# One-hot products of the spread step in three bf16 parts instead of one float32 product, with tokens innermost

## The reference, cut to what matters

```
eid  = i1 * 128 + i2                      # 8 heads x 16 choices = 128 experts per token
gate = softmax(best_s)
act  = gelu(einsum('thkd,td->thk', u[eid], x))
out  = einsum('thk,thkd->td', gate * act, v[eid])
```

## Time and profile before

| what | before |
|---|---|
| median of 3 runs | 4023.95 us (4020.21 to 4025.05) |
| the profiled execution, its own time | 4031.59 us |
| its span in the profile | 4029.8 us |
| granted TensorE clock, mean over the span | 0.932 |
| busy: PE, weight loads, VectorE, ScalarE, GpSimd | 3728.5, 2386.4, 2323.1, 1266.1, 658.0 us |

### The profile page before, as it was taken

The page is one execution under the profiler, slowest core; times in us unless marked ns, Lnnn a source line. Parts: engine busy times, 40 slices in busy tenths (PEclk is TensorE's granted clock), DMA queues, the critical chain, the costliest instruction groups (busy, mean ns, idle before and its releaser), DMA issues.

```text
span 4029.8 us, 48913 instructions
## 1 busy us (share of the span) xinstructions
PE 3728.5 (93%) x14086; PEld 2386.4 (59%) x14086; DVE 2323.1 (58%) x4748; ACT 1266.1 (31%) x3367; POOL 658.0 (16%) x602
## 2 busy tenths in 40 slices
PE   7977999789999999997998899799589999999997
PEld 3443583576677777663444444347476677777764
DVE  1072696579877655664123400258978977755556
ACT  1141010357655454001011100101156755545201
POOL 0000001123433222220000000000113333311221
PEclk9988999669999999998997999899758999999998
DMA  3101148559999877993211112213657999977897
GB/s 131 64 20 52 63 169 362 198 204 388 379 392 400 342 298 299 396 383 133 73 63 47 42 73 73 84 61 120 258 188 289 386 377 394 391 300 301 343 384 284
DMA packets 129888, 926.81 MB, mean 230 GB/s; under 512 B 14800, under 2 KB 15744, under 8 KB 18184
## 3 DMA queue, kind: packets, MB, share of 16 engines
q0 software_dynamic: 73728, 536.90, 32.8%
q1 hardware_dynamic: 52368, 377.51, 24.4%
q10 hardware_dynamic: 3704, 11.36, 0.8%
HBM read 923.59 MB, written 2.12 MB: 230 GB/s over the span
## 4 chain that ended last, share of the span: by engine, by line
PE 86%; ACT 5%; DVE 5%; issue 2%; DMA 2%; ACTq 0%; DVEq 0%; POOL 0%; POOLq 0%; SPq 0%
PE proj L646 21%; PE proj L429 16%; PE obk L637 16%; PE tps L594 11%; PE proj L421 10%; PE proj L608 5%; ACT hot L920 2%; PE proj L578 2%; ACT hot L923 1%; DMA wring<-in_slabs 1%; PE tps L394 1%; PE obk L745 1%; DMA ring<-in_experts,idx 1%; DVE stat L1186 0%; PE proj L735 0%
## 5 line engine op out<-in xcount | busy, mean ns | idle before, releaser
L646 PE MATMUL proj<-wring,hT 128*128 128x512 f32 x2048 | 943.3, 604 | 1.8 <-DVE hT L1391 1.8
L374 POOL DMA_INDIRECT ring<-in_experts,idx x512 | 635.5, 1241 | 1766.1 <-DVE xn L1365 1655.9
L637 PE MATMUL obk<-hT,wring 128*128 128x256 f32 x3072 | 694.2, 379 | 0.0
L637 PEld LDWEIGHTS obk<-hT,wring 128*128 128x128 f32 x3072 | 583.5, 190 | 159.5 <-issue 89.5
L594 PEld LDWEIGHTS tps<-hT,hot 128*128 128x128 f32 x4096 | 601.0, 226 | 123.6 <-ACT hot L923 61.0
L594 PE MATMUL tps<-hT,hot 128*128 128x32 f32 x4096 | 597.8, 304 | 74.7 <-ACT hot L923 49.4
L1365 DVE SCALAR_TENSOR_TENSOR xn<-ring,coef,xn 128x1024 f32<-128x1024 f32 x512 | 628.7, 1280 | 22.4 <-DVE coef L1355 1.2
L1348 DVE SCALAR_TENSOR_TENSOR ring<-ring,xn 128x1024 f32<-128x1024 f32 x512 | 601.0, 1221 | 7.7 <-DMA ring<-in_experts,idx 7.6
L646 PEld LDWEIGHTS proj<-wring,hT 128*128 128x128 f32 x2048 | 377.0, 192 | 379.4 <-issue 372.6
L429 PE MATMUL proj<-hT,wring 128*128 128x512 f32 x1280 | 561.0, 596 | 9.2 <-DMA ring<-in_keys 5.2
L920 ACT ACTIVATE hot<-iota_sb,table 128x128 f32<-128x128 f32 x1792 | 567.1, 390 | 2.5 <-issue 1.3
(11 more groups left out here) (228 smaller groups left out, 2134.5 us busy)
## 6 DMA issues: line engine op xcount, KB each, us to landing
wring<-in_slabs SPq DMA_DIRECT2D x356, 1024.0 KB
ring<-in_experts,idx POOLq DMA_INDIRECT x512
x_res<-in_x SPq DMA_DIRECT2D x1, 2048.0 KB, 9.9
ring<-in_keys ACTq DMA_DIRECT2D x2, 1024.0 KB, 6.9
out<-x_res SPq DMA_DIRECT2D x4, 512.0 KB, 2.6
ring<-ada_rows ACTq DMA_DIRECT2D x1, 1536.0 KB, 6.3
ring<-in_norm_pre ACTq DMA_DIRECT2D x2, 512.0 KB, 7.2
ring<-ada_rows ACTq DMA_DIRECT2D x1, 1024.0 KB
```

Source lines behind the costliest of these rows:

```text
L374: pool.indirect_dma_start(rows[:, r, :], None, d[f"experts{layer + 1}"], bass.IndirectOffsetOnAxis(idx[:, k, r:r + 1], 0)).then_inc(row[r] ...
L637: m = pe.matmul(obk[:, j % 2, 0:DT], wring[:, k, at + c * P:at + (c + 1) * P], hT[:, c, GB * P:T], start=(c == 0), stop=(c == DC - 1))
L646: m = pe.matmul(proj[:, 2 * b + c, :], coef_t[:, j % 2, b * P:(b + 1) * P], wring[:, k, at + c * 512:at + (c + 1) * 512], start=False, sto ...
```

## The change

The spread's one matmul in float32 per token becomes three in bf16 that add up in PSUM. The one-hots are exact in bf16; the gate is split into three bf16 numbers whose sum is the float32 gate (`gate_parts`). Keys, gate parts and `iota` are kept in bf16; `iota8` is `iota` repeated for eight tokens. All one-hot tiles are laid out with the eight tokens innermost, so a token's weights and columns are read at a step of eight bf16 elements (16 bytes). `hot2` gets two buffers of a whole group instead of two single halves. In the lone spread VectorE writes all of `hot2`; in the chunks ScalarE still does, with eight activations into a step of 16 bytes and one relu over 1024. `key_numbers` now reads its iota out of `iota8`, at that same step. The diff, cut to its core:

```diff
-SG = 4
+PARTS = 3
-HOT2 = SGROUPS + (CHUNKS - 1) * SGROUPS * 2
+HOT2 = (CHUNKS - 1) * SGROUPS
...
-        table = sb("table", [P, 4, DT])
-        hot2 = sb("hot2", [P, 2, SG, NK])
+        iota8 = sb("iota8", [P, NK, TG], BF16)
+        keys = sb("keys", [P, 2 + PARTS, DT], BF16)
+        away = sb("away", [P, DT])
+        hot2 = sb("hot2", [P, 2, NK, TG], BF16)
...
-        hot1 = hT[:, 4:6, 0:TG * CK].rearrange("p k (t n) -> p k t n", t=TG)
+        hot1 = hT[:, 4:4 + PARTS, 0:TG * CK].bitcast(BF16).rearrange("p c (k n t) -> p c k n t", k=2, t=TG)
+        onehot1 = hT[:, 7, 0:TG * CK].bitcast(BF16).rearrange("p (k n t) -> p k n t", k=2, t=TG)
...
+                if hot2_count is not None:
+                    pe.wait_ge(hot2_ready, hot2_count)
                 pe.wait_ge(spread_free, grp + 1)
-                for half in range(2):
-                    if hot2_counts[half] is not None:
-                        pe.wait_ge(hot2_ready, hot2_counts[half])
-                    for t in range(SG):
-                        at = (half * SG + t) * CK
-                        m = pe.matmul(tps[:, k, at:at + CK], hot2[:, half, t, :], hot1[:, k, half * SG + t, :], start=True, stop=True)
-                    m.then_inc(spread_done, 1)
+                for t in range(TG):
+                    for c in range(PARTS):
+                        m = pe.matmul(tps[:, k, t * CK:(t + 1) * CK], hot2[:, k, :, t], hot1[:, c, k, :, t],
+                                      start=(c == 0), stop=(c == PARTS - 1))
+                m.then_inc(spread_done, 1)
...
-            def hot2_half(layer, c, g, half, token, count):
-                act.wait_ge(spread_done, g * 2 + ((layer * CHUNKS + c) * SGROUPS * 2 + half + 3))
-                for t in range(SG):
-                    i = act.activation(hot2[:, half, t, :], iota[:, :], ACT.Abs, bias=table[:, 3, bass.ds(token + (half * SG + t), 1)])
+            def hot2_group(layer, c, g, k, token, count):
+                act.wait_ge(spread_done, g + ((layer * CHUNKS + c) * SGROUPS + 1))
+                for t in range(TG):
+                    i = act.activation(hot2[:, k, :, t], iota8[:, :, t], ACT.Abs, bias=away[:, bass.ds(token + t, 1)])
                 i.then_inc(away_set, 1)
                 act.wait_ge(away_set, count)
-                act.activation(hot2[:, half, :, :], hot2[:, half, :, :], ACT.Relu, bias=1.0, scale=-1.0).then_inc(hot2_ready, 1)
+                act.activation(hot2[:, k, :, :], hot2[:, k, :, :], ACT.Relu, bias=1.0, scale=-1.0).then_inc(hot2_ready, 1)
...
                 with act.Fori(0, ROUNDS) as it:
-                        hot2_half(layer, 0, n, 1, token, n + (layer * HOT2 + 1))
                         spread_take(layer, 0, n, g % 2, token)
...
-                                hot2_half(layer, c + 1, tile, 0, token, made)
-                                hot2_half(layer, c + 1, tile, 1, token, made + 1)
+                                hot2_group(layer, c + 1, tile, j % 2, token, tile + (layer * HOT2 + c * SGROUPS + 1))
...
+            v.wait_ge(in_cst, 32)
+            v.tensor_copy(iota8[:, :, :], bcast(iota, 2, [P, NK, TG]))
             v.memset(silz[:, :, :], 0.0)
...
-                link(v.tensor_tensor(onehot, bcast(half_f, 3, grid), iota[:, 0:K].unsqueeze(1).unsqueeze(1).to_broadcast(grid),
+                link(v.tensor_tensor(onehot, bcast(half_f, 3, grid), iota8[:, 0:K, 0].unsqueeze(1).unsqueeze(1).to_broadcast(grid),
...
+            def gate_parts(job):
+                for b in range(TB - GB):
+                    at = slice(b * P, (b + 1) * P)
+                    i = v.tensor_tensor(rest[:, at], tps[:, (job + b) % 2, 2 * P:3 * P], keys[:, 2, at], ALU.subtract)
+                link(i)
+                link(v.tensor_copy(keys[:, 3, :], rest))
+                link(v.tensor_tensor(keys[:, 4, :], rest, keys[:, 3, :], ALU.subtract))
...
-                v.wait_ge(spread_done, g * 2 + (first * 2 + 2))
-                v.tensor_tensor(hot1[:, k, :, :], iota[:, c * CK:(c + 1) * CK].unsqueeze(1).to_broadcast([P, TG, CK]),
-                                bcast(table[:, 0, tok], 2, [P, TG, CK]), ALU.is_equal).then_inc(hot1_set, 1)
+                v.wait_ge(spread_done, g + (first + 1))
+                v.tensor_tensor(onehot1[:, k, :, :], iota8[:, c * CK:(c + 1) * CK, :], bcast(keys[:, 0, tok], 1, [P, CK, TG]),
+                                ALU.is_equal).then_inc(hot1_set, 1)
                 if both:
-                    v.wait_ge(spread_done, g * 2 + (first * 2 + 3))
-                    v.tensor_tensor(hot2[:, 0, :, :], iota[:, :].unsqueeze(1).to_broadcast([P, SG, NK]),
-                                    bcast(table[:, 1, bass.ds(token, SG)], 2, [P, SG, NK]), ALU.is_equal)
+                    v.tensor_tensor(hot2[:, k, :, :], iota8[:, :, :], bcast(keys[:, 1, tok], 1, [P, NK, TG]), ALU.is_equal)
                 v.wait_ge(hot1_set, g + (first + 1))
-                v.tensor_tensor(hot1[:, k, :, :], hot1[:, k, :, :], bcast(table[:, 2, tok], 2, [P, TG, CK]),
-                                ALU.mult).then_inc(hot_ready, 1)
+                v.tensor_tensor(hot1[:, :, k, :, :], bcast(onehot1[:, k, :, :], 1, [P, PARTS, CK, TG]),
+                                bcast(keys[:, 2:2 + PARTS, tok], 2, [P, PARTS, CK, TG]), ALU.mult).then_inc(hot_ready, 1)
...
                 v.wait_ge(tr_free, job + 2)
+                gate_parts(job)
```

More of the change, by code:

```diff
@@ L129, in build @@
         tri = sb("tri_sb", [P, P])
-        iota = sb("iota_sb", [P, NK])
+        iota8 = sb("iota8", [P, NK, TG], BF16)
         zeros = sb("zeros", [1, P + 512], BF16)
@@ L157, in build @@
         first_z = part(ring, NRING + NSPREAD // 2, CK * DT).rearrange("p (i t) -> p i t", t=DT)
-        hot1 = hT[:, 4:6, 0:TG * CK].rearrange("p k (t n) -> p k t n", t=TG)
+        hot1 = hT[:, 4:4 + PARTS, 0:TG * CK].bitcast(BF16).rearrange("p c (k n t) -> p c k n t", k=2, t=TG)
+        onehot1 = hT[:, 7, 0:TG * CK].bitcast(BF16).rearrange("p (k n t) -> p k n t", k=2, t=TG)
+        rest = hT[:, 7, 0:DT]
+        iota = gate[:, 0:NK // GB, :].rearrange("p s b -> p (s b)")
         dqT = part(ring, 0, 2048).rearrange("p (c t) -> p c t", c=4)
@@ L548, in key_scores @@
                             s = pe.matmul(bank[:, g % 2, tb * P:(tb + 1) * P], qT[:, g % 4, tb * P:(tb + 1) * P],
-                                          keys(it, g), start=True, stop=True)
+                                          sub_keys(it, g), start=True, stop=True)
                         s.then_inc(key_done, 1)
@@ L559, in route, with sub_keys @@
                     key_scores(7)
-            def keys(it, g):
+            def sub_keys(it, g):
                 return subk[:, bass.ds(it * 8 + g, 1), :].rearrange("p g n -> p (g n)")
@@ L583, in modulation, with spread_group @@
                 m.then_inc(mm_done, 4)
-            def spread_group(grp, k, hot2_counts):
+            def spread_group(grp, k, hot2_count=None):
                 pe.wait_ge(hot_ready, grp + 1)
+                if hot2_count is not None:
+                    pe.wait_ge(hot2_ready, hot2_count)
                 pe.wait_ge(spread_free, grp + 1)
-                for half in range(2):
-                    if hot2_counts[half] is not None:
-                        pe.wait_ge(hot2_ready, hot2_counts[half])
-                    for t in range(SG):
-                        at = (half * SG + t) * CK
-                        m = pe.matmul(tps[:, k, at:at + CK], hot2[:, half, t, :], hot1[:, k, half * SG + t, :], start=True, stop=True)
-                    m.then_inc(spread_done, 1)
+                for t in range(TG):
[3 more added lines that the diff above has]
+                m.then_inc(spread_done, 1)
             def first_dots(layer, first):
@@ L621, in experts @@
                     for g in range(RGROUPS):
-                        n = it * RGROUPS + g
-                        spread_group(n + layer * CHUNKS * SGROUPS, g % 2, (None, n + (layer * HOT2 + 1)))
+                        spread_group(it * RGROUPS + (layer * CHUNKS * SGROUPS + g), g % 2)
                 def spread_step(it, c, j):
@@ L628, in spread_step @@
                         n = it * BODY + j
-                        made = n * 2 + (layer * HOT2 + SGROUPS + (c - 1) * SGROUPS * 2 + 1)
-                        spread_group(n + (layer * CHUNKS + c) * SGROUPS, j % 2, (made, made + 1))
+                        spread_group(n + (layer * CHUNKS + c) * SGROUPS, j % 2, n + (layer * HOT2 + (c - 1) * SGROUPS + 1))
                 def dots_tile(tile, j):
@@ L787, in _ @@
                 act.dma_start(t, d[n]).then_inc(in_g1, 16)
-            for t, n in ((ident[:, :], "ident"), (iota[:, :], "iota")):
+            for t, n in ((ident[:, :], "ident"), (iota, "iota")):
                 act.dma_start(t, d[n]).then_inc(in_cst, 16)
@@ L968, in experts @@
                     bank = tps[:, (job + b) % 2, :].rearrange("p (c t) -> p c t", c=4)
```

(12 more changed lines are left out.)

2 lines of the change are left out of this document (1 added, 1 removed).

## The result

The changed kernel takes 4158.43 us (median of 4 runs, 4148.56 to 4166.86) against 4023.14 us before (the three runs of the table and one more): a ratio of 1.0326 with a 95% interval of 1.0311 to 1.0341. It is 3.3% slower. The forecast was 3996 us, faster, with a range of 3880 to 4200; the time lies in the range, but on the other side of no change.

What follows compares the result with a forecast made beforehand. TensorE was taken to bound chunks 1 and 2, ScalarE's chain tied with TensorE chunk 0, a three-engine chain the lone spread. -70 + 67 - 17 - 20 + 8 + 4 = -28 us took 4023.95 to 3996; range 3880 to 4200.

Steps and rivals of the forecast that it cites:

- The cost of a step of 16 bytes: 0.73 ns for every element VectorE or ScalarE reads or writes at that step, from a VectorE row; other end 0.
- part 3: ScalarE in the chunks: chunk 0's turn 6.35 us against 5.31, 67 us more; no cost in chunks 1 and 2.
- part 1: TensorE in the spread: 24 pairs at 61 ns, 0.32 us less a group; chunk 2 20 us less, chunk 1 17.
- rival B: Strided bf16 costs TensorE in spread_group what float32 did, 111 ns a pair: +259 us, 4283; chance 0.23.
- Rival A: The step costs nothing: a TensorE pair takes some 40 ns, -140 us, 3884; chance 0.22.
- Part 2: The lone spread: VectorE sets the pace at 3.23 us a group, 0.1 of it for waits; 70 us less.
- Rival C: VectorE takes one bf16 element per cycle, so one-hots cost 420 + 1220 + 950 ns: +39, 4063 us; chance 0.15.
- Part 4: The rest: key_numbers' strided iota 8 us more, covered by VectorE's wait in the first layer; setup 4 us more.

Runs made afterwards that it cites:

- flat_both: Changed kernel with ScalarE reading a flat iota and writing hot2 flat, TensorE reading those weights flat in the chunks: 3946.56 us, 0.9806 of the kernel before.
- moving_flat: As flat_both, but TensorE's moving operand is 32 elements side by side (wrong elements, same work): 3879.32 us.
- columns_16: As flat_both, but each matmul of the spread moves 16 columns in place of 32: 3885.51 us.
- weights_step: Against flat_both: weights read at a 16-byte step in the chunks, moving operand flat (wrong elements), ScalarE writing at the step: 4144.16 us.
- late_flat: As ahead, but in chunks 1 and 2 VectorE lays hot1 out flat per token and TensorE reads both operands flat: 3837.96 us, 0.9538 of the kernel before.
- ahead: As flat_both, with hot2 made one group ahead and key_numbers reading a flat iota: 3902.72 us, 0.9695 of the kernel before.
- halves: As flat_both, with key_numbers reading a flat iota and hot2 handed over in two halves of four tokens: 3935.04 us, 0.9775 of the kernel before.

## Why the prediction was wrong

**The step that failed** is the price taken under "The cost of a step of 16 bytes": 0.73 ns for every element that ScalarE reads or writes at the step, from VectorE's L1391. A write at that step lengthened the activation by 662 ns (1055 against 393), 5.2 ns an element, and moved the next one's start from 0.29 to 0.54 us on average, 2.0 ns an element. In part 3 that makes 4.88 us for eight activations in place of 3.17, 1.71 us a turn, or 109 us over 64 turns: chunk 0 missed its forecast by 111 (178 for 67). L1391 reads at a step and writes flat; it bounded a read and said nothing of a write. I gave 0 as the other end of the price on ScalarE, and nothing above; that end was missing, and none of the rivals held a dearer ScalarE.

**The cover that was named and gone.** Part 3 said that in chunks 1 and 2 ScalarE's 5.4 us lie beside 6.89 us of matmuls and cost nothing. With 1.71 us more they are 7.1, and that cover is used up. The stage of chunk 1 grew by 34 us where 17 less were forecast, and TensorE's longest waits there are for `hot1` (7.6 us in the first layer); flat_both, with the step taken from ScalarE and from TensorE's weights, has it at 548 for both layers, 7 under the kernel before. So ScalarE's length is shown as the cause, but the path is not: in chunk 2 ScalarE has the same work per tile and TensorE stays full (269.53 of 269.70 us). Chunk 1 differs by its third unit of rows per eight tiles, with VectorE busy for 217 us against 158; that a later gelu delays `hot1` only behind a VectorE so full is my reading, and no run tests it. In chunk 2 the tile went from 8.67 to 8.45 us: 0.22 for the 0.32 of part 1, the pitch being 62 ns for 61 and 0.07 us a group going to its two ends.

**What was right.** Part 1: the pitch, 60 to 62 ns for 61. Its working holds for the columns, by moving_flat and columns_16: 1.75 ns a column and 4 a pair, where VectorE's strided price gave 1.77 and 4. But there was luck in it. Nothing had shown that VectorE's price would hold for TensorE, and no run shows the 107 ns of column time from which the 4 came. And part 1 took the weight load at 96 ns, without a step: at the step it takes 164 ns and by itself sets the same 60 ns (weights_step), hidden here behind the columns. So rival B (111 ns) did not come. Rival A's free step did not either; a pair without any step is at 25 ns, cheaper than its 40. Part 2: the lone spread is held by VectorE; its 32 comparisons (L1384) start at 743.63 to 840.84, 3.14 us a group, without the 0.1 that I had added for waits. That makes 76 of the 82 us; the other 6 lie at the ends of the stage. Rival C did not come: in bf16 with both inputs running along the row, 256 and 1024 elements take 287 and 682 ns, 0.51 ns an element, against 1.05 in float32 (420 and 690 ns for 256 and 512), half as much. The Trainium skill (VectorE: DVE Perf Modes, section The perf-mode tier table) has twice the rate there, and the trace agrees with these numbers. Rival C's price was right for another layout: 958 ns for 768 elements (late_flat), 950 in rival C. Part 4: the routing of the second layer lost 8 us, as said, and ahead and halves, whose `key_numbers` reads flat, have the comparison back at 2293 ns.

**A cover that did not hold.** The +14 for the +12 of part 4 is in part luck. The 58.82 us of VectorE's wait were to cover `key_numbers` in the first layer, but the lone spread began 6.8 us late there (745.05 for 738.25), and 741.32 and 740.01 in ahead and halves show that the step was most of it. GpSimd's first fetch, which waits for VectorE's routing, was issued at 596.91 in place of 589.94, and TensorE's `modulation`, for which VectorE waits by way of the transposes, ended 5.5 us later (733.55 for 728.08), having waited for its weights. That the later fetches slowed those weights is likely and not tested. Two readings are slightly off, and neither moves the sum: the last four tokens took 0.97 us and not 0.93, and the slope of L1374 and L1378 is 1.05 ns.

**The rule of the lines.** The Trainium skill (Advanced Engine Details and Errata, section Memory Cachelines) has a penalty where each access goes to another line of 16 bytes. The runs agree in kind for TensorE's two operands and for ScalarE's reads, all tried at 16 bytes. For ScalarE's writes they agree in the pace, which is 0.29 us up to a step of 8 bytes and 0.54 at 16. They do not in the duration: it grows from a step of 4 bytes on (430, 556 and 1055 ns at 4, 8 and 16 bytes against 393 flat), where several elements still share a line.

**The hand-over.** Part 3 counted the lost overlap of the half-wise hand-over as a cost. The runs leave that open: with halves put back, the fast turns did become 5.1 us, but the others 6.1 and more, and the stage did not move (192 us for 191). Making `hot2` a group ahead did move it, by 10 us a layer.

## What to carry to other kernels

Before a layout is turned so that one engine runs at twice its rate, every other engine that reads or writes that tile is to be priced at the new step, reads and writes apart; the nearest row must be of the same engine and the same direction, or the range must be open upwards. Here one activation's output at a step of 16 bytes cost more than all that the layout won, and laying the same tile out flat for its writer turned +3.3% into -1.9%. The layout need not be one for the whole kernel: tokens innermost where VectorE is full, flat where TensorE is, gave -4.6%.

## What the runs showed of the hardware that was not expected

ScalarE's output at a step: durations of 393, 430, 556 and 1055 ns for 128 bf16 elements at 2, 4, 8 and 16 bytes, with starts 0.29 us apart for the first three and 0.54 for the last. TensorE's small bf16 pair: 25 ns with both operands flat at the full clock, 60 with either at a step of 16 bytes, 62 with both. The strided pair hardly knows the clock: 60 to 62 ns in the chunks at a granted clock of 1.00 (2.4 GHz) and in the lone spread at 0.50 (1.2 GHz), where the float32 records went from 111 to 213 ns. And the transfers reached 412 GB/s at a share of 1.00 (late_flat, chunk 1), in step with the 390 that stood at 0.95 before.
